# Layer 1 of a two-layer transformer block on one core: the compression's products, bank copies and softmax put in other places

## The reference

```python
q, kc, vc, ks, vs, kw, vw, gt = split(h @ w_in)          # 1024, then six of 256, then 48 columns
q = rms_norm(q, q_norm);  q_rot = partial_rope(q, positions)   # 16 heads of 64
kc = rms_norm(nsa_compress(kc, pos_k, w1_k, w2_k), kcmp_norm)
vc = nsa_compress(vc, pos_v, w1_v, w2_v)
# nsa_compress: 15 overlapping blocks of 32 rows, silu((x[blocks] + pos) @ w1) @ w2
ks = partial_rope(rms_norm(ks, ksel_norm), positions);  kw = ... (the same)
p_c = masked_softmax(q . kc)      # compressed branch, un-rotated q, 15 blocks
# selected branch (q_rot . ks) and window branch (q_rot . kw) over the 256 tokens
o = gate0 * (p_c @ vc) + gate1 * (p_s @ vs) + gate2 * (p_w @ vw)
x = x + o @ w_out
x = x + memory_cross_attention(x, mem);  x = x + swiglu(x)
```

## Time and profile before

| | us |
|---|---|
| median of 3 runs | 1560.9 (1560.6 to 1562.7) |
| profiled execution, its own time | 1562.7 |
| its span | 1560.8 |
| PE busy | 1395.4 (89%) |
| DVE busy | 1070.6 (69%) |
| ACT busy | 746.4 (48%) |
| POOL busy | 87.9 (6%) |
| granted clock of PE, mean | 0.936 |

### The profile page before, as it was taken

One profiled execution on the slowest core, in us unless ns is written; L12 is line 12 of the kernel. 1 busy time (PEld: TensorE's weight loads), 2 busy tenths in 40 slices (PEclk: granted clock), 3 DMA queues, 4 the chain that ended last, 5 costly groups with the idle time before them and its releaser, 6 DMA issues.

```text
span 1560.8 us, 18380 instructions
## 1 busy us (share of the span) xinstructions
PE 1395.4 (89%) x6769; PEld 1152.0 (74%) x6769; DVE 1070.6 (69%) x1745; ACT 746.4 (48%) x925; POOL 87.9 (6%) x177
## 2 busy tenths in 40 slices
PE   6879697999989868888999988988879999999996
PEld 4767486788878755676888867876768787888884
DVE  4885776655556766585555558776568888979795
ACT  5344443444435216544444443463336767676673
POOL 0000301000000004301000000510000000000000
PEclk9999798999999767999999999999979999999997
DMA  6444033555654300042655545443539797989790
GB/s 227 157 137 147 1 107 105 180 188 183 192 163 152 124 14 2 20 156 69 201 189 188 188 128 167 156 162 124 216 134 372 264 355 282 355 285 356 282 356 29
DMA packets 123509, 277.62 MB, mean 178 GB/s; under 512 B 15382, under 2 KB 68780, under 8 KB 108076
## 3 DMA queue, kind: packets, MB, share of 16 engines
q1 hardware_dynamic: 121168, 275.99, 51.8%
q10 hardware_dynamic: 2268, 0.65, 0.2%
HBM read 275.57 MB, written 1.05 MB: 177 GB/s over the span
## 4 chain that ended last, share of the span: by engine, by line
PE 71%; DVE 17%; ACT 5%; issue 3%; DMA 2%; ACTq 0%; POOL 0%; DVEq 0%; SPq 0%
PE bank L1991 20%; PE bank L1993 19%; PE bank L1992 19%; DVE t_wlo L1174 2%; PE bank L2415 2%; DVE t_wlo L1185 2%; DMA t_raw<-in_ab_w_in 1%; ACT t_whi L766 1%; PE bank L2082 1%; PE bank L2264 1%; PE bank L2065 1%; PE bank L2105 1%; PE bank L2090 1%; DVE t_z L1331 1%; PE bank L2056 1%
## 5 line engine op out<-in xcount | busy, mean ns | idle before, releaser
L1174 DVE TENSOR_TENSOR t_wlo<-t_raw,t_whi 128x2048 fp32r<-128x2048 f32 (+3 forms) x144 | 315.9, 2203 | 147.3 <-ACT t_whi L753 145.1
L1991 PE MATMUL bank<-t_whi,t_ahi 128*128 128x512 f32 (+3 forms) x832 | 332.3, 399 | 32.1 <-DVE t_wlo L1174 13.9
L753 ACT ACTIVATE t_whi<-t_raw 128x2048 fp32r<-128x2048 f32 (+3 forms) x144 | 263.6, 1840 | 155.3 <-PE bank L1993 140.3
L1991 PE MATMUL bank<-t_whi,t_bhi 128*128 128x512 f32 (+1 forms) x800 | 314.3, 393 | 21.7 <-DVE t_z L1880 6.6
L1992 PE MATMUL bank<-t_wlo,t_ahi 128*128 128x512 f32 (+3 forms) x832 | 327.0, 393 | 0.0
L1993 PE MATMUL bank<-t_whi,t_alo 128*128 128x512 f32 (+3 forms) x832 | 326.2, 392 | 0.0
L1993 PE MATMUL bank<-t_whi,t_blo 128*128 128x512 f32 (+1 forms) x800 | 308.1, 385 | 0.0
L1992 PE MATMUL bank<-t_wlo,t_bhi 128*128 128x512 f32 (+1 forms) x800 | 307.9, 385 | 0.0
L1991 PEld LDWEIGHTS bank<-t_whi,t_ahi 128*128 128x128 f32 x832 | 160.3, 193 | 70.7 <-issue 29.1
L1991 PEld LDWEIGHTS bank<-t_whi,t_bhi 128*128 128x128 f32 x800 | 152.5, 191 | 53.5 <-issue 19.0
L1993 PEld LDWEIGHTS bank<-t_whi,t_alo 128*128 128x128 f32 x832 | 160.3, 193 | 32.6
(11 more groups left out here) (372 smaller groups left out, 1431.1 us busy)
## 6 DMA issues: line engine op xcount, KB each, us to landing
t_raw<-in_ffn_w_in SPq DMA_DIRECT2D x88, 512.0 KB, 4.7
t_raw<-in_ffn_w_out SPq DMA_DIRECT2D x22, 1024.0 KB, 4.9
t_raw<-in_w_in SPq DMA_DIRECT2D x18, 1024.0 KB, 5.1
t_raw<-in_exp_w_up SPq DMA_DIRECT2D x18, 1024.0 KB, 6.7
t_raw<-in_exp_w_down SPq DMA_DIRECT2D x18, 1024.0 KB, 6.8
t_raw<-in_exp_w_gate SPq DMA_DIRECT2D x15, 1024.0 KB, 7.2
t_memo<-in_exp_w_gate SPq DMA_DIRECT2D x13, 1024.0 KB, 7.3
t_feat<-in_exp_w_up SPq DMA_DIRECT2D x13, 1024.0 KB, 7.0
```

The costliest lines, as they stand in the source:

```text
L753: act.activation(whi[slot][:, 0:n], raw[slot][:, 0:n], ACT.Copy).then_inc(hi_done, 1)
L1174: dve.tensor_tensor(wlo[slot][:, 0:n], raw[slot][:, 0:n], whi[slot][:, 0:n].bitcast(F32), ALU.subtract).then_inc(lo_done, 1)
L1991: pe.matmul(dst, lhi, rhi_, start=start, stop=False)
```

## The change

1. W1 moves up: it stood after q1's product, and stands now between the first and the second group of q0's product. Its two loops are exchanged, so that matmuls of the upper and lower half of the rows alternate. W2 moves from the third hook of `vg` to the first group's hook of q1.
2. The banks of layer 1's turns are copied by ACT (new `turn_copy`) instead of DVE, but for one of q1's and one of the compressed probabilities' (`q1turn2`, `cmpturn2`). ACT also copies `VBLK`.
3. GpSimd clears three buffers, multiplies the keys' gains and makes all rotations (`rope` in its block, 26 instructions with the gains).
4. The order around `vg`: compressed key's transpose in group 0's hook, rotated keys in group 1's, rotated q0 in group 2's, q1's turn behind the product. The compressed scores of both chunks are 32 matmuls in one row with the halves alternating, chunk 1 into banks of `G` (new `cmp_bank`).
5. The softmax of the compressed scores moves into the attention (DVE at t=1 and t=3), its transposes too (PE at t=2), and q1's rotated turns (t=0). The attention takes heads 0 to 7 first; bank numbers and the out product's order follow.
6. In `vg`'s product ACT and DVE no longer split ahead (`ahead=0`): the out product's first two units are split in the attention at t=6 and t=10.
7. In both layers' memory attention DVE's two low parts for `mo` move: one to t=4, one behind the attention.

```diff
-                s["cmpkvturn"] = plan.turn(2, 0, 1)
...
+                s["cmpkvturn"] = plan.turn(2, 1, 0)
...
-        CS, CP = (shared[:, 512:1024], z[:, 5728:6240]), (shared[:, 1024:1536], z[:, 6240:6752])
+        CS, CP = (shared[:, 512:1024], shared[:, 1024:1536]), (Z1[:, 0, 0:512], Z1[:, 1, 0:512])
...
+        def cmp_bank(c, half_):
+
+            return (SCB if c == 0 else G[2 * ((L[1]["vg"][0].index + 1) % 2):])[half_]
...
-            for h0 in (8, 10, 0, 2):
+            for h0 in (0, 2, 8, 10):
...
+            pool.wait_ge(flag("keys_normed"), 1)
...
+            step(rope(keys_[0][0], ROPET1))
+            rope(keys_[1][0], ROPET1).then_inc(flag("keys_roped"), 1)
+            pool.wait_ge(flag("keys_roped"), 1)
+            for n, last in ((0, L[1]["q0turn"] + 2), (1, L[1]["q1turn2"] + 1)):
+                pool.wait_ge(flag("q_plain1"), n + 1)
+                pool.wait_ge(turned, last)
+                rope(heads(Z1, NQ + 512 * n, 8, DH), ROPET1).then_inc(flag("q_roped1"), 1)
...
-            def product(slabs, dst, src=bank_of, scale=True):
+            def product(slabs, dst, src=bank_of, scale=True, ahead=2):
...
-                    split_to(s.end + 2)
+                    split_to(s.end + ahead)
...
+            def turn_copy(n, dst):
+
+                act.wait_ge(turned, n + 1)
+                act.activation(dst, turn_bank(n)[:, 0:dst.shape[1]], ACT.Copy).then_inc(turn_act, 1)
...
+                        if t == 0:
+                            for b in range(2):
+                                turn_copy(s["qrturn2"] + b, feat[:, 3072 + 512 * b:3584 + 512 * b])
+                        if t == 2:
+                            turn_copy(s["cmpturn"], CPT[0])
+                        if t in (6, 10):
+                            split_to(s["vg"][-1].end + (t - 2) // 4)
...
+                    if t == 4:
+                        split_to(first_out)
...
-                product(s["mq"][1:2], zm, scale=None)
-                mem_attention(l, s["mheads"], s["mqturn"] + 1, (0, 1))
+                product(s["mq"][1:2], zm, scale=None, ahead=0)
+                mem_attention(l, s["mheads"], s["mqturn"] + 1, (0, 1), s["mo"][0].end)
...
+                        if group == 13:
+                            emptied(s["posturn"] + 1)
+                            pe.wait_ge(flag("cmp_weights_in"), 32)
+                            for j in range(CMP_LEN):
+                                for n in range(2):
...
-                    for n in range(2):
-                        r = slice(DH * n, DH * n + DH)
-                        for j in range(CMP_LEN):
...
-                        for h in range(16):
+                        for h in (h0 + 4 * half_ + i for h0 in (0, 8) for i in range(4) for half_ in range(2)):
...
+                    pe.wait_ge(flag("cmp_read"), 1)
+                    attention(items1(), s["heads"], between=compressed)
```

More of the change, by code:

```diff
@@ new lines, in _ @@
+                    split_to(s["q0"][-1].end + 1)
+                    act.wait_ge(flag("cmp_hidden"), 1)
+                    act.activation(HIT, HID, ACT.Tanh, scale=0.5).then_inc(flag("cmp_tanh"), 1)
+                    product(s["q0"], z1_dst, z1_src)
+                    head_squares([(heads(Z1, NQ, 8, DH), SQ1["q0"])], s["q0"], "q0")
+                    split_to(s["q1"][-1].end + 2)
+                    act.wait_ge(flag("cmp_k_read"), 1)
+                    for j in range(4):
+                        r = slice(32 * j, 32 * j + 32)
+                        ins = act.activation(VBLK[r, :, j, :], SCB[1][r, 128:384].rearrange("p (g d) -> p g d", g=4), ACT.Copy)
@@ new lines, in _ @@
+                    ins.then_inc(flag("cmp_v_ready"), 1)
+                    for b in range(2):
+                        turn_copy(s["q0turn"] + b, feat[:, 512 * b:512 * b + 512])
+                    product(s["q1"], z1_dst, z1_src)
+                    head_squares([(heads(Z1, NQ + 512, 8, DH), SQ1["q1"])], s["q1"], "q1")
+                    turn_copy(s["kcturn"], KCT)
+                    for b, dst in enumerate((feat[:, 4096:4608], KWT, feat[:, 2048:2560], feat[:, 2560:3072])):
+                        turn_copy(s["qrturn"] + b, dst)
@@ L1062, in _ @@
+                    product(s["vg"], z1_dst, z1_src, ahead=0)
                     act.wait_ge(slab_act, s["vg"][-1].done_act)
@@ L1283, in head_norm @@
                     at_ += C * n
[L1284 removed]
+                rsqrt(at_ + more, d)
                 at_ = 0
@@ L1291, in head_norm @@
                 step(ins)
+                if not parts[0][2]:
+                    return
                 for _, _, gs in parts:
@@ L1729, in _ @@
+                    head_norm([(SQ1["q1"], vq[1], [(vq[1], gains[:, N_NQ, :])])], DH, "q1")
+                    dve.sem_inc(flag("q_plain1"), 1)
+                    product(s["vg"], z1_dst, z1_src, ahead=0)
+                    turns(s["q1turn2"], 1, lambda b: feat[:, 1536:2048])
                     dve.wait_ge(flag("gates_tanh"), 1)
@@ L1765, in _ @@
+                    attention(items1(), s["heads"], (2, 3, 0, 1), True, between=compressed)
                 product(s["out"][0:1], None)
@@ L2068, in turns, with attention @@
                     emptied(base + len(jobs) // 2)
-            def attention(items, run):
+            def attention(items, run, between=None):
                 n = run.n
```

244 lines of the change are left out of this document (125 added, 119 removed).

## The result

The changed kernel takes 1528.1 us (median of 4 runs, 1527.2 to 1528.6); the kernel before took 1561.8 in the same rounds. The ratio is 0.978 (95% interval 0.977 to 0.980). The prediction said 1529. The profiled execution took 1528.6 us, 34.1 less than the profiled one of before; its span is 1526.9.

The account below looks back on a forecast made before the run. PE's feeding bounds the kernel (71% of the chain), with DVE work in series in layer 1. Layer 1's terms (-28.4) and the memory attentions (-5.2) sum to -33.6, from 1562.7 to 1529 us; range 1519 to 1546.

Parts of the forecast that it names:

- W1: Compression's first product: with alternating halves each pair costs one pass, so 8.6 us instead of 16.2.
- the scores at 589.96: Attention's first scores, cited as evidence that halves overlap: four matmuls in 1.23 us, against 1.8 without overlap.
- DVE out of the path up to the scores: q0 to the compressed scores: DVE work moved to GpSimd and ACT or covered by W1; +3.7, then -28.4 us.
- The softmax in the attention: Compressed scores and softmax: -17.4 us before attention's start, +5.7 in steps 0 to 4, which carry both softmaxes.
- The two splits: Attention at t=6 and t=10: high and low parts cost +5.5 us, bounds zero and 8.4.
- The clock: +2.5 us at half clock: 1.5 in q0's matmuls behind W1, 1.0 in some attention steps.
- The memory attentions: Both layers: PE's wait for DVE's two low parts goes, 2 x -2.6 = -5.2 us.
- A: Halves don't overlap in W1 and the compressed scores: 1537 to 1542, taken as 1540 us; chance 0.08.
- B: Attention absorbs: splits in series +2.9, steps behind softmaxes late by 2, GpSimd holding DVE +2; about 1538 us; chance 0.17.
- C: Clock stays at 1.2 GHz after W1 for seven groups: 19 us more, 1548; chance 0.05.
- D: GpSimd becomes the bound on keys and rotations: gain gone from 2.6 us per instruction on, 1563 or slower; chance 0.02.
- E: Better case: the splits and the clock cost nothing, 1521 us; chance 0.10.

Follow-up runs that it names:

- scores_by_half: The changed kernel with the compressed scores ordered by half inside each token chunk instead of alternating; 1537.0 us, 0.983 of before.
- splits_back: The changed kernel with the out product's first two units' high and low parts back in vg's product, none in the attention; 1530.4 us, 0.980 of before.
- softmax_before: The changed kernel with the compressed softmax, its transposes and q1's rotated turns ahead of the attention's first step again; 1530.5 us, 0.979 of before.
- before_w1_alternating: The kernel before with W1's two loops exchanged so that halves alternate, nothing else; 1558.5 us, 0.996 of before.
- the control: The changed kernel measured and profiled once more, nothing altered; 1529.8 us, 0.978 of before.
- w1_loops_back: The changed kernel with W1's two loops in the old order, one half of the rows then the other; 1539.7 us, 0.985 of before.
- hi_lo_early: The changed kernel with both high parts and DVE's first low part moved before the attention, the second low part in step 6; 1522.1 us, 0.974 of before.
- hi_early: The changed kernel with ACT's two high parts moved before the compressed softmax, DVE's low parts left in steps 6 and 10; 1526.2 us, 0.976 of before.

## Why the prediction was right

The terms, read from the two profiled executions at the same instructions of PE (us):

| stretch | before | after | change | predicted |
|---|---|---|---|---|
| q0's first group to q1's end | 25.9 | 30.0 | +4.1 | +3.7 |
| q1's end to the scores | 39.0 | 10.6 | -28.4 | -28.4 |
| scores to attention's start | 21.3 | 3.6 | -17.8 | -17.4 |
| steps 0 to 4 | 6.2 | 12.6 | +6.3 | +5.7 |
| steps 4 to 14, two splits | 16.1 | 25.6 | +9.5 | +5.5 |
| steps 14 to out; clock | 41.4 | 38.9 | -2.5 | +2.5 |
| memory attentions | 43.6 | 37.9 | -5.6 | -5.2 |
| sum | | | -34.4 | -33.6 |

(The measured changes are formed before rounding. Of the predicted +2.5 for the clock, 1.5 belonged to q0, so to the first row.)

**W1.** Right in size and in cause. It took 8.45 us (8.6 predicted), and the experiment with the loops back puts all of it on the alternation. The 12 passes in the one microsecond of the earlier trace rows in which the half changes were the evidence, and the only one. The second, the scores at 589.96, doesn't come out as it was worked: as the order lists show, the x4 of that row are the recorded passes of two matmuls, not four matmuls of two passes each. By the prediction's own pitch four such passes are 0.9 us at half clock, and the next row starts 1.02 behind, so this row shows no overlap by that count.

**DVE out of the path up to the scores.** Right in every time: no wait in q0 and q1, scores at 540.5 (541.6 predicted), attention at 544.0 (545.5); the program was 1.5 us early at W1 already. (The parts that the prediction lists for q1's end to the scores add up to 39.7, not 39.0, since some are lengths and not pitches; the difference was taken from 39.0 and isn't touched.) But the credit was given to several parts at once. The experiments take it from GpSimd: with the rotations on DVE the stretch from W1 to the scores is 0.2 us longer. That ACT's bank copies were needed wasn't tried. The other part of the mechanism, which the prediction named in half a sentence, is W1's own cover: W1 gives DVE 8.5 us in which PE needs nothing of it. The alternation alone shows the opposite case, with 6.2 us of waits for DVE behind the shorter W1.

**The softmax in the attention.** The difference of the two terms (-17.4 and +5.7) was right, but read as a gain of weaving it would be wrong. DVE has most of the time from the scores to step 4 in both orders, and weaving itself is worth 3.1 to 3.4 us by the profiles, nothing that the medians tell. Of the 17.8, 3.5 are what scores_by_half gives back, its lower clock included; how the rest divides between the waits that stood between the scores and the bank copies that ACT took over wasn't tried apart.

**The two splits.** This term was mis-sized: 9.5 us instead of 5.5. splits_back divides the 9.5. With both splits out of the attention steps 4 to 14 take 17.4 us, so 8.2 are the splits', all of it in steps 8 to 14 (17.3 against 9.0). They stood almost wholly in series, at the prediction's own bound of 8.4; what failed is the step-by-step schedule, which let 3 of the 8.4 us fall into idle time. Two waits of 3.5 us are most of it, and between them PE goes on at a lower clock. PE's step 10 in the changed kernel, then in splits_back:

```profile
571.30:575.77 4.47, 4.47 (x29) 3.27 (x29) 2.33 (x13) 2.90 (x14) 2.69 (x7) 0.62 0.61 229
573.54:576.50 2.96, 2.96 (x31) 2.18 (x29) 2.36 (x13) 1.67 (x8) 2.15 (x6) 1.00 0.02 6
```

The other 1.3 us are not the splits' and had no term. Steps 4 to 8 take 8.3 us with or without them, against 6.7 before and 6.6 in softmax_before: behind the softmax in the steps before, PE's clock comes back later. Step 6 in the changed kernel, in splits_back and in the kernel before:

```profile
559.54:564.92 5.38, 5.38 (x28) 3.90 (x28) 2.47 (x13) 3.20 (x13) 2.30 (x6) 0.50 0.00 0
565.35:570.73 5.38, 5.38 (x28) 3.90 (x28) 2.47 (x13) 3.20 (x13) 2.30 (x6) 0.50 0.00 0
596.38:600.54 4.16, 4.16 (x28) 3.00 (x28) 2.41 (x13) 2.41 (x12) 2.30 (x6) 0.67 0.01 2
```

From 4 to 8 that is 1.65 us more; the steps from 8 on, without the splits, give 0.35 back.

**The clock.** The other mis-sized term, of the opposite sign, and this is why the sum came out. The 1.5 us for q0 behind W1 didn't come: W1 with alternation didn't bring the clock down, since the earlier trace rows were rows of the loop without it. The rest, which shows as -2.5 from step 14 on, is no effect of the change that these runs show. The same stretch in the kernel before, in before_w1_alternating and in the control:

```profile
609.90:651.30 41.40, 33.74 (x334) 24.99 (x332) 23.81 (x127) 23.36 (x87) 19.47 (x41) 0.92 0.00 1
609.30:647.70 38.40, 30.74 (x335) 22.93 (x333) 23.81 (x127) 23.37 (x87) 19.37 (x41) 1.00 0.00 1
583.80:625.95 42.15, 35.99 (x333) 27.21 (x333) 23.85 (x127) 24.34 (x93) 20.44 (x43) 0.85 0.04 13
```

With the attention of before it takes 41.4 or 38.4 us, with that of the change 38.9 or 42.1, in step with the clock. Read from the control's profile the term is +0.7 and the sum -31; the medians, over four executions each, gave 0.978 both times. So the 1 us between forecast and result is better than the working deserves: two terms were wrong by 4 and 5 us in opposite directions, and some 3 us of the second are the luck of the profiled pair.

**The memory attentions.** -2.3 and -3.4 against -2.6 each; the low part at t=4 cost nothing that the runs show.

**The rivals.** A (no overlap) is refuted for W1 and for the scores by w1_loops_back and scores_by_half, which also show its price: 10 us, and 4 by the stages to 7 by the medians. B (the attention absorbs) was right as a mechanism for 4 us: its +2.9 for splits in series came as 2.7, its 2 us behind the softmaxes as 1.7; its 2 us for GpSimd don't show. (Its terms as listed add up to 1536; for 1538 the 2 us must stand for each softmax.) C (clock low after W1) happened only with the loops back, and for 2.0 us. D (GpSimd the bound) was far off. E's free splits did not come in the changed kernel; with the parts put elsewhere (hi_lo_early) 7.1 of the 8.2 us came back in these steps, and 5.6 up to the out product.

## What to carry to other kernels

Matmuls that use half of the rows of PE cost about half here when neighbours use different halves (W1 8.4 against 16.2 us); look for a single place in the trace where the half changes, before rewriting the loop. A work item that needs two engines in series (a high part, then a low part) should have its first half in an earlier stage than its second: both in the same pipeline step cost 4.1 us each here, with the high parts moved out (hi_early) 1.4. A term read from one pair of profiles in a stretch with many waits can be off by 3 us through the clock alone; look at the granted clock on both sides, and profile one kernel twice. Before work is given to a slower engine, look whether the fast one is still on the path after the other edits: here it wasn't.

## What the runs showed of the hardware

With alternation the granted clock was 1.00 through W1's 8.4 us of small matmuls, at either place and in all eleven profiles; the same matmuls in one half's order were at 0.50 from 505.0 to 517.4, and at 0.61 on the mean in the kernel before. I had taken the clock's fall for a property of the small matmuls. For the compressed scores the runs don't show as much: alternating they ran at 1.00 in the changed kernel, but the clock fell to 0.52 halfway through in hi_lo_early, and in splits_back, where PE had stood for 4.99 us, they ran at 0.50 throughout and took 7.04 us. W1's pace without alternation was the same at either clock, that of the alternating scores was not (3.76 and 7.04). And the same kernel's last attention steps ran at 1.00 in one execution and 0.76 in another, 2.6 us apart, with equal busy times of DVE and ACT.
